# Where the C tiles stand in the second mixer's input projection

## The chip, the cores and the metric

The kernel runs on one core of a Trainium2 chip. One launch computes the whole step, and the metric is the device time of that launch in microseconds. Engines are named as in the profile: PE is TensorE's matrix multiply and PEld its weight load, DVE is VectorE, ACT is ScalarE, POOL is GpSimd and SP is the engine that issues most of the DMAs. In a profile row, "idle before <- X" says how long an engine stood still before the instruction, and who released it.

## What is computed

The reference is one inference step of a trunk with two layers: layer 0 mixes tokens with a long convolution (Hyena), layer 1 with a bidirectional Mamba-2 scan (SSD), and each is followed by an expert-choice mixture of experts. There are 128 context tokens and 1024 latent tokens, 9 tiles of 128 in all, with a model width of 1024. The change touches only the SSD mixer's input projection:

```python
proj = h @ in_w
z = proj[..., :SSD_D_INNER]
xbc = silu(_dwconv(proj[..., SSD_D_INNER:SSD_D_INNER + SSD_XBC], conv_w, conv_b))   # 5 taps along the tokens
dt_raw = proj[..., SSD_D_INNER + SSD_XBC:]
xh, bm, cm = split(xbc)            # 2048 columns of x, 4 groups x 128 of B, 4 groups x 128 of C
...
chunk_states = einsum('bcsgn,bcsgrp->bcgrpn', bm, xdt * decay_end[..., None])
s = s * dec[..., None, None] + st  # the recurrence over the chunks, forwards and backwards
y_off = einsum('bclgn,bcgrpn->bclgrp', cm, starts) * exp(a_cum)[..., None]
```

The states need B and x of a group, and not C. C and z are first used in the scan phase that comes afterwards.

## The kernel before

The program is a chain of phases with a barrier of all engines between them. `phase_ssd_in` is the projection. The output columns are cut into 40 tiles of 128 columns: 16 z tiles, 16 x tiles, 4 B tiles and 4 C tiles (`xbc_tile_of` numbers x as 0 to 15, B as 16 to 19, C as 20 to 23). They are worked through in the order q = 0 to 39. Three z tiles lead in. After them come four periods of nine tiles, one for each group g; `place(q)` gives the group and the position j in it. Position 0 is the group's B tile, positions 1 to 4 are its four x tiles, and what positions 5 to 8 hold is what the change is about. One tile is left over after the last period.

Work on a tile q, by engine:

- PE: 72 matmuls of 128x384 (`project`, recorded at L63, in the helper `product3`), in two halves with side work between (`middle(q)`) and behind (`end(q)`). Each product is made of three, from a leading and a trailing part of the weights and of h.
- A z tile: ACT evicts three banks with a SiLU in one instruction (`z_tile`, L3063), and POOL stores 576 KB to `z_dram` (L3337).
- An x, B or C tile: ACT evicts in three copies into a padded tile (L3072 to L3074) and computes the middle tap (L3079), DVE adds the other four taps one behind the other (`taps`, L3214), ACT takes the SiLU (L3087), and POOL stores 64 and 512 KB to `xbc_dram` (L3342, L3343). Of x and B tiles PE also makes transposes (`turn`, L2957), which ACT copies out (L3101, L3119).
- ACT and DVE split the weights of tile q+2 into their leading and trailing part (`lead`, L3058, and `rest`, L3205).

The states of a group run on the same engines as side work. At position 5, behind `taps(q)` and `rest(q+2)`, DVE decays the first state in both directions (`decay`, L3261) and weighs the x rows of the first chunk (`weigh`, L3248). In the middle of position 6 PE multiplies these with B (`contribute`, L2983); it waits there for `s_xw`, the semaphore that `weigh` raises. DVE then adds the product to the state (`add`, L3268), weighs the next chunk, and so on, two steps a tile: positions 6, 7 and 8 take steps 0 to 5, and position 0 of the next group takes step 6 and the context's own step (L2980, whose result ACT copies out at L3136 and SP stores in four DMAs at L2878).

The order on every engine is written out by hand: what an instruction waits for holds back all that is queued behind it on its engine. The phase ends when SP has seen all its stores land and POOL all of its own. Then the semaphores are cleared, all engines meet, and `phase_scan` begins with SP's first load (L3434).

Of the kernel before, what the change touches and what calls it, by code (L numbers as in the profile page):

```python
# [37 lines left out]
GROUPS = 4  # L38
XBC_TILES = 24
Z_TILES = 16  # L40
# [2632 lines left out]
LEAD_IN = 3  # L2673
# [5 lines left out]
def place(q):  # L2679

    return divmod(q - LEAD_IN, PERIOD)


def xbc_tile_of(q):

    if q < LEAD_IN:
        return None
    g, j = place(q)
    if g == GROUPS:
        return Z_TILES + 2 * GROUPS - 1  # L2690
    if j == 0:
        return Z_TILES + g
    if j <= 4:
        return 4 * g + j - 1
    if g == GROUPS - 1 and j >= 6:
        return Z_TILES + GROUPS + j - 6
    return None


def z_tile_of(q):  # L2700
    return q if q < LEAD_IN else LEAD_IN + 4 * place(q)[0] + place(q)[1] - 5


def tile_columns(q):
    x = xbc_tile_of(q)
    at = z_tile_of(q) * P if x is None else INNER + x * P
    return slice(at, at + P)


XBC_BEFORE = [sum(xbc_tile_of(p) is not None for p in range(q)) for q in range(TILES_IN + 1)]  # L2710

STORED_BEFORE = [sum(16 if xbc_tile_of(p) is None else 32 for p in range(q % 2, q, 2)) for q in range(TILES_IN + 2)]


# [36 lines left out]
def phase_ssd_in(nc, io, keep):  # L2751


    with ExitStack() as ctx:
# [91 lines left out]
        with nc.Block() as block:  # L2846
# [484 lines left out]
            @block.gpsimd  # L3331
            def _(pool):
                for q in range(TILES_IN):
                    x, s_done = xbc_tile_of(q), s_st[q % 2]
                    if x is None:
                        pool.wait_ge(s_ev, q + 1)
                        pool.dma_start(io["z_dram"][:, :, z_tile_of(q), :].rearrange("t p c -> p t c"),  # L3337
                                       out[:, q % 2, 0:TOK].rearrange("p (t c) -> p t c", c=P)).then_inc(s_done, 16)
                    else:
                        pool.wait_ge(s_si, XBC_BEFORE[q] + 1)  # L3340
                        group, at = (x // 4, x % 4) if x < Z_TILES else (x % 4, 4 + (x - Z_TILES) // 4)
                        pool.dma_start(io["xbc_dram"][0, :, group, at, :], out[:, q % 2, 0:P]).then_inc(s_done, 16)  # L3342
                        pool.dma_start(io["xbc_dram"][1:, :, group, at, :].rearrange("t p c -> p t c"),  # L3343
                                       out[:, q % 2, LAT_AT:].rearrange("p (t c) -> p t c", c=P)).then_inc(s_done, 16)
                    if q == LEAD_IN:
                        for n in range(3):
                            wait_taken(pool, U_ROWS + n)
                        pool.dma_start(io["row_dram"].rearrange("t r l -> r t l"),
                                       S(2).rearrange("p (t l) -> p t l", l=P)).then_inc(s_cr, 16)
                for b in range(2):  # L3350
                    pool.wait_ge(s_st[b], STORED_BEFORE[TILES_IN + b])
                pool.wait_ge(s_cr, 16)
# [507 lines left out]
```

## Time and profile before

| | us |
|---|---|
| median of 3 runs | 3690.69 (3690.11 to 3694.54) |
| the profiled execution's own time | 3688.76 |
| its span | 3687.0 |
| PE busy | 3384.2 (92%) |
| DVE busy | 1864.5 (51%) |
| ACT busy | 1278.0 (35%) |
| mean granted clock of TensorE | 0.951 of full speed |

The input projection lies between about 1790 and 2389 us of the span, the scan phase behind it. The granted clock is 1.00 where TensorE runs at 2.4 GHz and 0.50 at 1.2 GHz.

### The profile page before, as it was taken

The page shows a single profiled execution, that of the slowest core. Times are in us where ns is not written, and L with a number is a line of the kernel's source. Part 1 is how long each engine was busy: PE and PEld are TensorE (multiplying, and loading weights), DVE is VectorE, ACT ScalarE, POOL GpSimd, SP SyncE. Part 2 cuts the span into 40 slices and gives each one's busy share as a digit, 9 for nine tenths or more (in the row PEclk, how much of TensorE's full clock was granted, in tenths as well). Part 3 has the DMA queues.
Part 4 walks back from the last instruction along what each step waited for, and adds up shares of the span by engine and source line. Part 5 has one row for each costly group of instructions (what it writes and reads, how often), then busy time and mean ns, then how long its engine had stood idle before and what let it go on. Part 6 is the DMA issues. An engine that isn't in the chain of part 4 may idle for free. (4 is left out here: it accounts for less than half of the span.)

```text
span 3687.0 us, 58736 instructions
## 1 busy us (share of the span) xinstructions
PE 3384.2 (92%) x24055; PEld 2915.0 (79%) x24055; DVE 1864.5 (51%) x3039; ACT 1278.0 (35%) x2048; POOL 365.2 (10%) x356
## 2 busy tenths in 40 slices
PE   6999898977699999997899999789997499999998
PEld 5999674755599999996899999656664499999997
DVE  6333487765433333333455455599996533333334
ACT  4322323222133333333433233267664132232223
POOL 0000000000111111111010000000000011111111
PEclk8999898988799999998899999989998699999999
DMA  7666313254688888885143443497776488888887
GB/s 244 225 199 203 132 48 127 105 198 160 239 287 286 287 287 286 286 290 175 54 134 102 156 143 101 134 345 250 255 256 233 151 286 293 299 289 286 286 289 263
DMA packets 414015, 798.95 MB, mean 217 GB/s; under 512 B 21991, under 2 KB 108844, under 8 KB 412555
## 3 DMA queue, kind: packets, MB, share of 16 engines
q1 hardware_dynamic: 384940, 700.50, 54.1%
q0 software_dynamic: 28720, 96.31, 8.8%
q8 instruction: 102, 1.67, 0.2%
q14 instruction: 45, 0.37, 0.0%
q10 hardware_dynamic: 208, 0.10, 0.0%
HBM read 687.94 MB, written 108.90 MB: 216 GB/s over the span
## 5 line engine op out<-in xcount | busy, mean ns | idle before, releaser
L2438 PEld LDWEIGHTS moe_banks<-moe_xt,mix_ring 128*128 128x128 f32 x8192 | 1012.1, 191 | 5.7 <-issue 3.2
L2438 PE MATMUL moe_banks<-moe_xt,mix_ring 128*128 128x144 f32 x8192 | 1013.4, 287 | 3.1 <-ACT moe_xt L2482 3.1
L63 PE MATMUL ssd_banks<-h_leading,ssd_w_split 128*128 128x384 f32 x1920 | 417.3, 346 | 1.5 <-DVE ssd_w_split L3205 1.5
L2611 DVE TENSOR_TENSOR moe_hid<-moe_banks,moe_sg 128x128 f32<-128x128 f32 x256 | 74.6, 292 | 580.8 <-ACT moe_sg L2534 580.8
L2463 PE MATMUL moe_banks<-moe_down_parts,moe_hid_parts 128*128 128x512 f32 x1536 | 357.8, 392 | 0.0
L63 PEld LDWEIGHTS ssd_banks<-h_leading,ssd_w_split 128*128 128x128 f32 x1920 | 339.3, 189 | 16.1 <-issue 13.6
L2463 PEld LDWEIGHTS moe_banks<-moe_down_parts,moe_hid_parts 128*128 128x128 f32 x1536 | 285.9, 188 | 71.3 <-issue 13.2
L2554 DVE TENSOR_TENSOR moe_down_parts<-mix_ring,moe_down_parts 128x2048 fp32r<-128x2048 f32 x128 | 292.4, 2284 | 0.0
L3486 PE MATMUL scan_banks<-scan_w,scan_yc 128*128 128x512 f32 x576 | 255.0, 596 | 0.0
L2398 POOL DMA_INDIRECT x_dram<-moe_yc,mix_idx_quarter x128 | 166.3, 1299 | 830.7 <-DVE moe_yc L2622 801.5
L63 PE MATMUL hyin_early_banks<-h_leading,hyin_early_w_split 128*128 128x384 f32 x1152 | 245.0, 340 | 0.9 <-PEq L101 0.9
L2490 ACT ACTIVATE moe_down_parts<-mix_ring 128x2048 fp32r<-128x2048 f32 x128 | 242.9, 1897 | 0.0
L2534 ACT ACTIVATE moe_sg<-moe_banks 128x144 f32<-128x144 f32 x256 | 74.5, 291 | 427.2 <-PE moe_banks L2438 426.6
L63 PE MATMUL ssd_banks<-h_trailing,ssd_w_split 128*128 128x384 f32 x960 | 222.6, 338 | 0.0
L3214 DVE SCALAR_TENSOR_TENSOR ssdin_mid<-ssdin_pad,prm,ssdin_mid 128x1154 f32<-128x1154 f32 x96 | 136.4, 1421 | 156.5 <-ACT ssdin_mid L3079 154.0
L2534 ACT ACT_TABLE_LOAD x30 | 38.5, 1283 | 501.6 <-PE moe_banks L2438 501.6
L63 PEld LDWEIGHTS hyin_early_banks<-h_leading,hyin_early_w_split 128*128 128x128 f32 x1152 | 204.2, 189 | 2.8 <-issue 2.6
L3486 PEld LDWEIGHTS scan_banks<-scan_w,scan_yc 128*128 128x128 f32 x576 | 107.6, 192 | 122.3 <-issue 122.3
L2604 DVE SCALAR_TENSOR_TENSOR moe_yr<-moe_banks,mix_gate_lat,moe_g 128x512 f32<-128x512 f32 x64 | 48.0, 750 | 303.9 <-PE moe_banks L2463 298.8
L63 PEld LDWEIGHTS ssd_banks<-h_trailing,ssd_w_split 128*128 128x128 f32 x960 | 172.5, 189 | 0.0
L63 PE MATMUL hyin_early_banks<-h_trailing,hyin_early_w_split 128*128 128x384 f32 x576 | 137.3, 338 | 0.0
L1820 PE MATMUL hyout_banks<-hyout_w_parts,hyout_g_parts 128*128 128x512 f32 x432 | 104.4, 399 | 19.5 <-DVE hyout_g_parts L1856 19.5
(472 smaller groups left out, 4381.8 us busy)
## 6 DMA issues: line engine op xcount, KB each, us to landing
mix_ring<-in_moe_w_gate SPq DMA_DIRECT2D x64, 2048.0 KB, 8.0
mix_ring<-in_moe_w_up SPq DMA_DIRECT2D x64, 2048.0 KB, 12.9
mix_ring<-in_moe_w_down SPq DMA_DIRECT2D x64, 2048.0 KB, 8.7
early_ring<-in_ada_w SPq DMA_DIRECT2D x84, 512.0 KB, 6.6
scan_cum<-row_dram SPq DMA_DIRECT2D x36, 1024.0 KB, 6.6
ssd_w<-in_ssd_in_w SPq DMA_DIRECT2D x40, 512.0 KB, 4.2
s_dram<-ssdin_work SPq DMA_DIRECT2D x64, 256.0 KB, 3.6
scan_states<-s_dram SPq DMA_DIRECT2D x32, 512.0 KB, 7.9
```

What stands on the lines that cost most here:

```text
L63: ins = pe.matmul(out(piece), w_at(w[a], k), h_k(h[b], k, piece), start=(k == 0 and a == 0 and b == 0), stop=(k == KD - 1 and a == 1))
L1820: ins = pe.matmul(pb[:, 2 * (t % 2) + half, :], g_parts[:, t % 2, a, k, :], w_parts[:, b, k, half * HALF:(half + 1) * HALF], start=(k == 0 ...
L2398: pool.indirect_dma_start(io["x_dram"].rearrange("t (a c) -> (t a) c", a=4), bass.IndirectOffsetOnAxis(ap=keep["idx_quarter"][:, j, e:e + ...
L2438: ins = pe.matmul(pb[:, 2 * (f % 2) + j, 0:SLOTS], ring[:, 2 * half + j, k, col:col + P], xt[:, k, :], start=(k == 0), stop=(k == KD - 1))
L2463: ins = pe.matmul(pb[:, LAT_BANK[half], :], hid_parts[:, a, k, :], wd[:, half, b, k, :], start=(k == 0 and a + b == 0), stop=(k == KD - 1 ...
L2490: act.activation(wd[:, half, 0, ks, :], ring[:, 4 + half, ks, :], ACT.Copy).then_inc(s_wh, 1)
L2534: act.activation(sg[:, f % 2, :], pb[:, 2 * (f % 2), 0:SLOTS], ACT.Silu).then_inc(s_sg, 1)
L2554: dve.tensor_tensor(wd[:, half, 1, ks, :], ring[:, 4 + half, ks, :], wd[:, half, 0, ks, :].bitcast(F32), ALU.subtract).then_inc(s_wl, 1)
L2604: dve.scalar_tensor_tensor(yr[:, cols], pb[:, LAT_BANK[half], :], column("gate_lat", e), g2[:, cols], ALU.mult, ALU.mult).then_inc(s_yr, 1)
L2611: dve.tensor_tensor(hid[:, f % 2, :], up[:, 0:CAP_LAT], sg[:, f % 2, 0:CAP_LAT], ALU.mult).then_inc(s_hid, 1)
L3214: ins = dve.scalar_tensor_tensor(mid[:, b, :], pad[:, b, tap:tap + GAPPED], prm[:, 0, at:at + 1], mid[:, b, :], ALU.mult, ALU.add)
L3486: ins = pe.matmul(pb[:, out_bank(t) + half, :], yc[:, n % RING, j, :], w[:, k, half * HALF:(half + 1) * HALF], start=(k == 0), stop=(k == ...
```

## The change

Two functions are edited, `xbc_tile_of` and `z_tile_of`; all engines read the order of the tiles from them.

```diff
     g, j = place(q)
     if g == GROUPS:
-        return Z_TILES + 2 * GROUPS - 1
+        return None
     if j == 0:
         return Z_TILES + g
     if j <= 4:
         return 4 * g + j - 1
-    if g == GROUPS - 1 and j >= 6:
-        return Z_TILES + GROUPS + j - 6
+    if j == 5:
+        return Z_TILES + GROUPS + g
     return None
 
 
 def z_tile_of(q):
-    return q if q < LEAD_IN else LEAD_IN + 4 * place(q)[0] + place(q)[1] - 5
+    return sum(xbc_tile_of(p) is None for p in range(q))
```

Before, a period was B, x, x, x, x and four z tiles, except in the last group, where one z tile was followed by C, C, C and, as the left-over tile q = 39, the fourth C. Now each period is B, x, x, x, x, C and three z tiles, and q = 39 is a z tile. The counts are the same, 16 z tiles and 24 others, and so are all the instructions of PE, in number and kind.

On DVE, the end of the first group before (L3214 are the taps of a tile, L3205 the split of weights, L3261 and L3248 the first decay and the first weighing of the group's states, L3268 their first sum):

```order
L3214 SCALAR_TENSOR_TENSOR ssdin_mid<-ssdin_pad,prm,ssdin_mid 128x1154 x4
L3205 TENSOR_TENSOR ssd_w_split<-ssd_w,ssd_w_split 128x1024 x2
L3261 TENSOR_TENSOR ssdin_work<-ssdin_work,rates 128x512 x2
L3248 TENSOR_TENSOR ssdin_xw<-ssdin_work,rates 128x512 x2
L3268 TENSOR_TENSOR ssdin_work<-ssdin_work,ssd_banks 128x512 x2
```

and the same place after the change:

```order
L3214 SCALAR_TENSOR_TENSOR ssdin_mid<-ssdin_pad,prm,ssdin_mid 128x1154 x4
L3205 TENSOR_TENSOR ssd_w_split<-ssd_w,ssd_w_split 128x1024
L3214 SCALAR_TENSOR_TENSOR ssdin_mid<-ssdin_pad,prm,ssdin_mid 128x1154 x4
L3205 TENSOR_TENSOR ssd_w_split<-ssd_w,ssd_w_split 128x1024
L3261 TENSOR_TENSOR ssdin_work<-ssdin_work,rates 128x512 x2
L3248 TENSOR_TENSOR ssdin_xw<-ssdin_work,rates 128x512 x2
L3268 TENSOR_TENSOR ssdin_work<-ssdin_work,ssd_banks 128x512 x2
```

Four more taps stand ahead of the second weight split, and so ahead of the first decay and weighing. This holds in each of the four groups.

On ACT, the end of the phase before (L3072 to L3074 and L3079 evict a tile with taps, L3087 is its SiLU, L3136 the copy of the context's states):

```order
L3087 ACTIVATE ssdin_out<-ssdin_mid 128x1154
L3072 ACTIVATE ssdin_pad<-ssd_banks 128x128
L3073 ACTIVATE ssdin_pad<-ssd_banks 128x256
L3074 ACTIVATE ssdin_pad<-ssd_banks 128x768
L3079 ACTIVATE ssdin_mid<-ssdin_pad,prm 128x1154
L3136 ACTIVATE ssdin_ctx_state<-ssd_banks 128x512 x2
L3087 ACTIVATE ssdin_out<-ssdin_mid 128x1154
```

and after the change, where L3063 is the eviction of a z tile and L3058 ACT's part of a weight split:

```order
L3063 ACTIVATE ssdin_out<-ssd_banks 128x1152
L3058 ACTIVATE ssd_w_split<-ssd_w 128x1024
L3063 ACTIVATE ssdin_out<-ssd_banks 128x1152
L3058 ACTIVATE ssd_w_split<-ssd_w 128x1024
L3063 ACTIVATE ssdin_out<-ssd_banks 128x1152 x2
L3136 ACTIVATE ssdin_ctx_state<-ssd_banks 128x512 x2
```

The last tile's chain of eviction, taps and SiLU has become one eviction, and the copies of the context's states are the last thing that ACT does in the phase. POOL's last two stores to `xbc_dram` have become one to `z_dram`.

## Rows read from the trace of the kernel before

**Rows 1.** Windows (length; busy us PE, PEld, DVE, ACT, POOL; clock, DMA, GB/s)

```profile
2242.00:2312.00 70.00, 70.00 (x424) 69.69 (x423) 34.09 (x25) 31.04 (x47) 8.25 (x11) 1.00 0.31 96
2312.00:2344.00 32.00, 32.00 (x163) 28.13 (x162) 24.35 (x33) 8.61 (x13) 1.48 (x2) 1.00 0.50 176
```

**Rows 2.** Timeline of PE, last group (start us, duration us, engine, line, operation)

```profile
2316.01 1.88 PE L2983 MATMUL ssd_banks<-ssdin_xw,ssdin_brow 128*128 128x512 f32 x4
```

**Rows 3.** Timeline of DVE, positions 4 and 5 of the last group

```profile
2298.14 5.79 DVE L3214 SCALAR_TENSOR_TENSOR ssdin_mid<-ssdin_pad,prm,ssdin_mid 128x1154 f32<-128x1154 f32 x4 [7.02 <-ACT ssdin_mid L3079]
2303.84 1.22 DVE L3205 TENSOR_TENSOR ssd_w_split<-ssd_w,ssd_w_split 128x1024 fp32r<-128x1024 f32 x1
2312.06 1.23 DVE L3205 TENSOR_TENSOR ssd_w_split<-ssd_w,ssd_w_split 128x1024 fp32r<-128x1024 f32 x1 [7.00 <-ACT ssd_w_split L3058]
2313.20 1.29 DVE L3261 TENSOR_TENSOR ssdin_work<-ssdin_work,rates 128x512 f32<-128x512 f32 x2
2314.40 1.29 DVE L3248 TENSOR_TENSOR ssdin_xw<-ssdin_work,rates 128x512 f32<-128x512 f32 x2
```

**Rows 4.** Timeline of ACT, the same two positions

```profile
2295.46 0.28 ACT L3072 ACTIVATE ssdin_pad<-ssd_banks 128x128 f32<-128x128 f32 x1 [3.62 <-PE ssd_banks L63]
2308.97 1.14 ACT L3063 ACTIVATE ssdin_out<-ssd_banks 128x1152 f32<-128x1152 f32 x1 [3.67 <-PE ssd_banks L63]
```

**Rows 5.** Timeline of PE, start of the projection

```profile
1806.23 1.96 PE L2926 MATMUL ssd_banks<-tri,ssdin_work 64*128 64x64 f32 x16 [4.03 <-DVE ssdin_ones L3315]
...
1811.83 2.12 PE L63 MATMUL ssd_banks<-h_leading,ssd_w_split 128*128 128x384 f32 x6
1813.75 1.16 PE L63 MATMUL ssd_banks<-h_trailing,ssd_w_split 128*128 128x384 f32 x3
...
1816.73 1.20 PE L63 MATMUL ssd_banks<-h_leading,ssd_w_split 128*128 128x384 f32 x6
1817.77 0.68 PE L63 MATMUL ssd_banks<-h_trailing,ssd_w_split 128*128 128x384 f32 x3
```

**Rows 6.** Windows around three idle spells of PE

```profile
1802.20:1805.40 3.20, 0.00 (x0) 0.00 (x0) 3.10 (x4) 0.00 (x0) 0.00 (x0) 1.00 0.00 0
1805.40:1815.70 10.30, 7.92 (x35) 7.74 (x36) 4.29 (x12) 4.04 (x4) 2.18 (x2) 0.50 0.60 173
...
456.20:460.60 4.40, 0.03 (x1) 0.03 (x1) 4.33 (x5) 1.06 (x2) 0.00 (x0) 1.00 0.50 120
460.60:464.00 3.40, 3.40 (x8) 2.72 (x9) 3.40 (x4) 1.97 (x2) 0.00 (x0) 0.50 0.00 0
...
777.60:781.50 3.90, 3.90 (x9) 3.13 (x10) 3.90 (x4) 3.42 (x4) 0.00 (x0) 0.50 1.04 348
```

**Rows 7.** Timeline of ACT and POOL, end of the projection and one z tile

```profile
2372.07 0.28 ACT L3072 ACTIVATE ssdin_pad<-ssd_banks 128x128 f32<-128x128 f32 x1 [4.24 <-PE ssd_banks L63]
...
2374.61 1.06 ACT L3136 ACTIVATE ssdin_ctx_state<-ssd_banks 128x512 f32<-128x512 f32 x2
...
2310.39 0.99 POOL L3337 DMA_DIRECT2D z_dram<-ssdin_out  x1 [3.52 <-ACT ssdin_out L3063]
...
2382.57 0.90 POOL L3343 DMA_DIRECT2D xbc_dram<-ssdin_out  x1
```

**Rows 8.** Timeline of PE and SP, end of the projection

```profile
2371.87 1.95 PE L2980 MATMUL ssd_banks<-ssdin_brow,ssdin_xw 128*128 128x128 f32 x16
...
2375.21 2.90 SPq L2878 DMA_DIRECT2D out_new_state<-ssdin_ctx_state  x4
2389.64 0.38 SPq L3434 DMA_DIRECT2D scan_cum<-row_dram  x1
```

**Rows 9.** DMA issues, 2360 to 2389 us, then the whole run (last: us to landing)

```profile
xbc_dram<-ssdin_out POOLq DMA_DIRECT2D x2, 512.0 KB, 3.8
out_new_state<-ssdin_ctx_state SPq DMA_DIRECT2D x4, 128.0 KB, 2.4
...
z_dram<-ssdin_out POOLq DMA_DIRECT2D x16, 576.0 KB, 4.9
```

## The prediction

> **What bounds the kernel now.** I read the windows by stage first. In the last group, where the tiles still stand in their old order, PE is busy all the time at full clock: 70.00 of 70 us up to the first z tile's end, and 32.00 of 32 us where the C tiles begin [rows 1]. DVE has 24 of 32 us in the densest part and 34 of 70 in the other. So PE sets the time of the projection, its instructions aren't changed, and the only ways for this edit to move the time are to make PE stand still inside the phase, or to change what lies between PE's last matmul and the first load of the next phase. I therefore read two places in the timelines: the point at which PE first needs a group's weighed rows, and the end of the phase.
>
> At the first place PE comes to the contribution L2983 at 2316.01, with no idle time before it [rows 2]. DVE weighs both directions from 2314.40 for 1.29 us, so until 2315.69 [rows 3]. The slack is 0.3 us. At the second place PE is done at 2373.8 (2371.87 + 1.95), and SP's first load of the scan goes out at 2389.64 [rows 8]: 15.8 us in which PE has nothing.
>
> **Part 1: the C tile in position 5, four times.** The z tile there is evicted from 2308.97 [rows 4]. A tile with taps is evicted from the same point of its tile (position 4: 2295.46), and its taps begin on DVE at 2298.14, 2.68 us later [rows 3, 4]. So the C tile's taps begin at 2308.97 + 2.68 = 2311.65. From the taps' start to that of the weight split behind them is 5.70 us (2303.84 - 2298.14), from there to the decay 1.14 (2313.20 - 2312.06), from there to the weighing 1.20 (2314.40 - 2313.20), and the first of the two weighings takes half of 1.29, 0.65 [rows 3]. That ends at 2311.65 + 5.70 + 1.14 + 1.20 + 0.65 = 2320.3. PE wants it at 2316.0 and gets it 4.3 us later. The second weighing ends at 2321.0, when the first direction's two matmuls are just done, and adds nothing. ACT isn't late: its two copies of the last x tile come before its SiLU, and what it does behind that SiLU (the third copy, some 0.3 us) is over at about 2319, since the taps end at 2317.4.
>
> What is queued behind the waiting matmul on PE is the second half of position 6 and all that follows. PE has no slack in the phase to make it up in, since it is at 100% on both sides of the place; DVE, ACT and the weight loads move back with it. So 4.3 us a group are lost, four times: 17.2 us. Bounds: not under 3.7 (if the eviction or the copies in between go half a microsecond faster than in position 4), not over 5.0.
>
> **Part 2: the clock after such a wait.** The trace has a stall like this in the same phase: PE stood idle for 4.03 us before 1806.23 [rows 5], the clock was 1.00 up to 1805.4 and 0.50 until 1815.7, with 7.92 us of PE busy in it [rows 6]. Another, 4.4 us long, before 460.6: the clock then was 0.50 for 3.4 us of dense matmuls. At 777.6 dense matmuls began at the low clock and it took 3.9 us to rise [rows 6]. At the low clock six matmuls of 384 columns are 1.92 us apart (1813.75 - 1811.83), at the full one 1.04 (1817.77 - 1816.73) [rows 5], so a busy microsecond at the low clock loses 1 - 1.04/1.92 = 0.46 us. Bounds for each stall: nothing, if the clock holds; 7.92 x 0.46 = 3.6 us, as at 1806. There the first thing behind the idle time was 16 small transposes and a second wait of PE; here real matmuls follow without a hole, as at 460.6 and 777.6. I take 3.4 to 3.9 us, 1.6 us lost in each, 6.4 in all, and keep 0 and 14.4 as ends.
>
> The Trainium skill, page "TensorE: Matmul & The Clock Gate", section "Why this matters for your kernels", warns of gaps of more than about 3 us between bursts of matmuls, which speaks against this change; its section "What you observe" puts the return to full speed at about 4 us of sustained matmuls. By that rule each stall would lose 4 x 0.46 = 1.8 us and the sum below would be 0.8 us more; by the row at 1806, where it took 10.3 us, it would be 8 us more.
>
> **Part 3: the C tiles leave positions 6 to 8 of the last group.** DVE has 3 x 5.8 us less there. PE was at 100% with them [rows 1], so nothing is gained: DVE's busy time was beside PE's.
>
> **Part 4: the end of the phase.** Before, PE's last product went through ACT's eviction (from 2372.07), four taps on DVE and the SiLU, and POOL issued the last store at 2382.57 [rows 7]; with 3.8 us to landing [rows 9] it was there at 2386.4, and SP's first load followed at 2389.64, 3.2 us on. Now the last tile is evicted at 2372.07 in 1.13 us, and POOL issues its store 1.42 us after ACT's start (2310.39 - 2308.97) [rows 4, 7], at 2373.5. With the run's median of 4.9 us for such a store [rows 9] it lands at 2378.4. The other end is SP's: the context's states. They were copied from 2374.61 [rows 7] and stored by four DMAs from 2375.21, 0.73 us each, the last at 2377.4 [rows 8], landing 2.4 us later [rows 9]. ACT can now copy the first direction right behind the eviction, at about 2373.1 instead of 2374.61, and the second when PE's last matmul is done, 2373.9. That moves the last landing from 2379.8 to 2378.3. So both ends come out at 2378.4 where 2386.4 was before: 8.0 us gained. What is late next is these two together. Bounds: 6.0 (each is 2 us later, because the two stores and the last states share the DMA engines) and 9.0 (an undisturbed store lands after 3.8 us and the copies go earlier).
>
> **The sum.** 17.2 + 6.4 - 8.0 = +15.6 us. Against the profiled execution's 3688.8 us that gives 3704.4. The median of the runs is 1.9 us above the profiled one, so a median would be 3706.3; I say 3706. Everything outside this phase is unchanged.
>
> **Rivals.**
> 1. The clock stays low after each stall as long as at 1806. For it: that is the only stall of this size in this phase [rows 5, 6]. Against it: what PE did behind it. 17.2 + 14.4 - 8.0 = +23.6, so 3714.
> 2. The clock holds. For it: PE is fully busy up to the wait and after it. Against it: both idle spells of 4.0 and 4.4 us were followed by a low clock [rows 6]. 17.2 - 8.0 = +9.2, so 3700.
> 3. The other side, faster: the first weighing is in time, and only the shorter end remains. Its place is PE's wait before L2983, its price nothing, and it would give -8.0, 3683. It decides once the wait is under 2.0 us a group (8.0/4). For that the four taps would have to cost under 2.3 us of delay, with 0.3 of slack; they take 5.79 [rows 3] and stand ahead of the weighing on an engine that works in order. I see nothing that would carry them past it.
> 4. No measurable change: the wait is there but about half as long, because the eviction, taps and weighing overlap better than position 4 shows, and the clock holds: 4 x 2.5 - 8.0 = +2, 3693.
>
> **How the numbers follow.** The forecast has 0.64, rival 1 0.14, rival 2 0.11, rival 3 0.05 and rival 4 0.06. A measurement of this kernel can tell about 0.2%, 7.4 us, from no change. Slower than that are the forecast, rival 1 and most of rival 2: 0.87. Within it are rival 4 and a little of rival 2: 0.08. Faster: 0.05. The range takes in rivals 1 and 2 with the bounds of the end of the phase: low is 4 x 3.7 - 8.0 = +6.8, so 3697; high is 17.2 + 14.4 - 6.0 = +25.6, so 3716.
>
> **What would show it.** In the profile of the changed kernel, PE waits about 4.3 us for DVE's L3248 in front of L2983, four times, 17 us in all, and there is no such wait before. The first weighing of a group begins 5.3 us later against the end of position 5's matmuls than before. After each of the four waits the granted clock is 0.50 for 3 to 4 us of work. The last z store is issued 1.4 us after ACT's last eviction, and SP's first load of the scan comes about 8 us after PE's last matmul instead of 15.8. The forecast is wrong if PE isn't seen waiting at L2983, if the clock is low for much longer than 4 us, or if the barrier still comes some 15 us behind PE because another store is the last to land.

## The result and the profile after

The changed kernel takes 3712.69 us (median, 3711.16 to 3714.27), the one before 3691.35 us in the same measurement: a ratio of 1.0058, with a 95% interval of 1.0046 to 1.0069. It is 21 us slower. The forecast was 3706, the range 3697 to 3716. The profiled execution took 3712.92 us, 24.2 us more than the profiled one of before.

The waits of PE on the second mixer's projection, in total, have a new entry (engine, line, waited for; us in total, times, longest):

```profile
PE ssd_banks L2983 <- DVE ssdin_xw L3248: 17.8, 4, 4.5
```

Before there was no such entry. The PE timeline of the changed kernel shows the first of the four, in answer to [rows 2], and where the next contribution comes:

```profile
1921.28 0.27 PE L2957 MATMUL ssd_banks<-tri,ssdin_out 128*128 128x128 f32 x1
1926.01 3.75 PE L2983 MATMUL ssd_banks<-ssdin_xw,ssdin_brow 128*128 128x512 f32 x4 [4.46 <-DVE ssdin_xw L3248]
...
1936.18 1.88 PE L2983 MATMUL ssd_banks<-ssdin_xw,ssdin_brow 128*128 128x512 f32 x4
```

Here the reader is to see two losses. The idle time is 4.46 us. Then the half tile up to the next contribution takes 10.17 us (1936.18 - 1926.01), where the same stretch before took 7.98, as before's PE timeline shows:

```profile
1919.14 0.27 PE L2957 MATMUL ssd_banks<-tri,ssdin_out 128*128 128x128 f32 x1
1919.25 1.88 PE L2983 MATMUL ssd_banks<-ssdin_xw,ssdin_brow 128*128 128x512 f32 x4
...
1927.23 1.88 PE L2983 MATMUL ssd_banks<-ssdin_xw,ssdin_brow 128*128 128x512 f32 x4
```

The contribution started 0.11 us after the start of the transpose in front of it, while that was still running; now it starts 4.73 us after it. So the wait moves all that follows by 4.62 us, a little more than the idle time.

DVE at the same place, in answer to [rows 3]. The taps of the C tile now stand between the last x tile's and the first weighing, which begins at 1925.07:

```profile
1917.02 5.79 DVE L3214 SCALAR_TENSOR_TENSOR ssdin_mid<-ssdin_pad,prm,ssdin_mid 128x1154 f32<-128x1154 f32 x4 [6.58 <-ACT ssdin_mid L3079]
1922.73 1.22 DVE L3205 TENSOR_TENSOR ssd_w_split<-ssd_w,ssd_w_split 128x1024 fp32r<-128x1024 f32 x1
1923.87 1.28 DVE L3261 TENSOR_TENSOR ssdin_work<-ssdin_work,rates 128x512 f32<-128x512 f32 x2
1925.07 1.28 DVE L3248 TENSOR_TENSOR ssdin_xw<-ssdin_work,rates 128x512 f32<-128x512 f32 x2
```

The windows of the changed kernel show the clock (length; busy us of PE, PEld, DVE, ACT, POOL; granted clock, DMA share, GB/s). The first lies in the first half of the first wait; the second, fourth, fifth and sixth are the low spells of the four groups, and the third is all that lies between the first two of them:

```profile
1921.60:1923.50 1.90, 0.00 (x0) 0.00 (x0) 1.90 (x2) 0.65 (x1) 0.00 (x0) 1.00 0.00 0
1923.50:1930.30 6.80, 4.29 (x7) 2.25 (x8) 4.04 (x7) 0.68 (x2) 1.45 (x2) 0.50 0.75 247
1930.30:2063.40 133.10, 130.31 (x740) 123.94 (x738) 68.83 (x73) 42.27 (x61) 10.32 (x14) 1.00 0.37 121
2063.50:2070.20 6.70, 5.13 (x9) 3.10 (x10) 3.94 (x8) 0.00 (x0) 1.33 (x2) 0.50 0.87 305
2203.50:2210.20 6.70, 5.65 (x11) 3.61 (x12) 3.95 (x8) 0.00 (x0) 0.80 (x1) 0.50 0.95 338
2343.40:2350.10 6.70, 5.88 (x12) 3.84 (x13) 3.94 (x7) 0.00 (x0) 0.57 (x1) 0.50 1.02 352
```

The clock falls to 1.2 GHz while PE still stands: 2.5 us before PE goes on at the first wait (1923.50 and 1926.01), 0.8 us before at the last. It stays low for some 6.8 us each time, and so 4.29 to 5.88 us of PE's work fall into it, 20.95 in all. The end of the phase, in answer to [rows 7, 8], from the timelines of PE, ACT, POOL and SP:

```profile
2403.02 1.95 PE L2980 MATMUL ssd_banks<-ssdin_brow,ssdin_xw 128*128 128x128 f32 x16
...
2403.22 1.13 ACT L3063 ACTIVATE ssdin_out<-ssd_banks 128x1152 f32<-128x1152 f32 x1 [14.83 <-PE ssd_banks L63]
...
2404.65 1.00 POOL L3337 DMA_DIRECT2D z_dram<-ssdin_out  x1 [14.97 <-ACT ssdin_out L3063]
...
2404.86 3.76 SPq L2878 DMA_DIRECT2D out_new_state<-ssdin_ctx_state  x4
2413.07 0.38 SPq L3434 DMA_DIRECT2D scan_cum<-row_dram  x1
```

From PE's end (2404.97) to the first load of the scan it is now 8.1 us, where it was 15.8.

These account for the profiled difference. From L2926 near the start (1808.48 after, 1806.23 before) to L2980 at the end (2403.02 after, 2371.87 before) PE takes 594.5 us where it took 565.6: 28.9 us more. Of that 18.5 are the waits (4 x 4.62). The low clock can be read by itself, from the start of each delayed contribution to that of the next one: 10.17, 10.57, 10.78 and 10.92 us where 7.98 was before, 10.5 us more in all, or 0.50 us for each of the 20.95 busy us. The two make 29.0. The end gives 7.7 back. The remaining 3.0 us lie outside: 2.3 are there before L2926 is reached, in phases that are the same in both, and 0.7 behind the first load. The medians, 21.3 us apart, agree with 28.9 - 7.7 = 21.2.

### The profile page after: what moved, and what is told of

Its sections match the earlier page's. It is cut to its first block and busy times, and to the rows that moved or that the text cites. A ratio compares the mean times of both kernels' runs of the same rounds, so it can differ in the third digit from the quotient of the medians.

```text
span 3711.1 us, 58736 instructions
## 1 busy us (share of the span) xinstructions
PE 3390.5 (91%) x24055; PEld 2918.4 (79%) x24055; DVE 1865.5 (50%) x3039; ACT 1277.4 (34%) x2048; POOL 365.5 (10%) x356
## 5 line engine op out<-in xcount | busy, mean ns | idle before, releaser
L63 PEld LDWEIGHTS ssd_banks<-h_leading,ssd_w_split 128*128 128x128 f32 x1920 | 341.6, 190 | 18.3 <-issue 15.8
L3214 DVE SCALAR_TENSOR_TENSOR ssdin_mid<-ssdin_pad,prm,ssdin_mid 128x1154 f32<-128x1154 f32 x96 | 136.5, 1422 | 177.1 <-ACT ssdin_mid L3079 174.6
## 6 DMA issues: line engine op xcount, KB each, us to landing
mix_ring<-in_moe_w_up SPq DMA_DIRECT2D x64, 2048.0 KB, 12.8
```

The costliest lines, as they stand in the source:

```text
L63: ins = pe.matmul(out(piece), w_at(w[a], k), h_k(h[b], k, piece), start=(k == 0 and a == 0 and b == 0), stop=(k == KD - 1 and a == 1))
L3214: ins = dve.scalar_tensor_tensor(mid[:, b, :], pad[:, b, tap:tap + GAPPED], prm[:, 0, at:at + 1], mid[:, b, :], ALU.mult, ALU.add)
```

## The experiments

All kernels below were timed beside the kernel before. Its median was 3690.42 us beside the first four and 3692.21 us beside the last four. Times of different occasions are compared by their distances from it.

**C in the seventh place, a z tile last.**

```diff
-    if j == 5:
+    if j == 6:
         return Z_TILES + GROUPS + g
```

> Each group's C tile in the seventh place (position 6) instead of the sixth; a z tile is still last. My theory: the loss comes from the taps that stand ahead of a group's first weighing, so PE doesn't wait at L2983 at all, the clock doesn't fall inside the projection, and only the shorter end of the phase is left: 7 to 8 us faster than before, about 3684. Rival A, more taps beside the side work cost wherever they stand (DVE is the denser for it): PE waits in position 6 or 7 and the time stays above 3695. Rival B, the shorter end was worth nothing and the whole difference lies elsewhere: 3691, as before.

Measured: 3681.84 us, ratio 0.9978 (0.9969 to 0.9987). PE's waits have no entry for L2983, and the stretch that holds all four groups is at full clock, with PE busy all but 1.1 us of it (a wait of 1.15 us at 1851, which the kernel before has as well):

```profile
1820.00:2372.00 552.00, 550.86 (x3118) 521.17 (x3118) 288.51 (x311) 175.59 (x254) 48.64 (x62) 1.00 0.39 126
```

One place further on, the taps stand behind the weighings of the steps, as DVE's timeline shows. The first weighing (1918.68) is again in time, and 5.8 us of taps start at 1933.19, where DVE's next deadline is the weight split for a tile still to come:

```profile
1916.33 1.23 DVE L3205 TENSOR_TENSOR ssd_w_split<-ssd_w,ssd_w_split 128x1024 fp32r<-128x1024 f32 x1 [7.00 <-ACT ssd_w_split L3058]
1917.47 1.29 DVE L3261 TENSOR_TENSOR ssdin_work<-ssdin_work,rates 128x512 f32<-128x512 f32 x2
1918.68 1.29 DVE L3248 TENSOR_TENSOR ssdin_xw<-ssdin_work,rates 128x512 f32<-128x512 f32 x2
...
1933.19 5.79 DVE L3214 SCALAR_TENSOR_TENSOR ssdin_mid<-ssdin_pad,prm,ssdin_mid 128x1154 f32<-128x1154 f32 x4
```

So the sixth place is what costs, and rival A (taps beside side work cost anywhere) is out. With the waits gone, the shorter end shows as a gain of 8 us, and rival B is out too. This version beats both kernels.

**C in the sixth place, the weighing first.**

```diff
+                    if q >= LEAD_IN and place(q)[1] == 5:
+                        ... decay and weigh, both directions
                     if xbc_tile_of(q) is not None:
                         taps(q)
                     rest(q + 2)
-                    if q >= LEAD_IN and place(q)[1] == 5:
-                        ... decay and weigh, both directions
```

On ACT, `middle(q + 1)` goes ahead of `silu(q)` in the same position: with the old order the third copy of the last x tile would wait for the taps, and PE for that copy's bank.

> The changed order of tiles (C in the sixth place), but in position 5 DVE does a group's first decay and weighing ahead of the taps of the C tile, and ACT does the middle work of the next tile ahead of that tile's SiLU. My theory: the queue order on DVE alone makes PE wait, so the wait at L2983 is gone or under 0.5 us a group, and the time is 6 to 8 us under before, about 3684 to 3686. Rival A, it is the C tile's own work in that place that is too much for DVE or ACT: some of the wait comes back at L2983 or later, at the weight split, and the time is between 3693 and 3713.

Measured: 3682.34 us, ratio 0.9980 (0.9971 to 0.9989), and no wait at L2983. The tiles stand exactly as in the changed kernel; only DVE's and ACT's order within one position differs. DVE's timeline shows that the weighing now waits for ACT's copies of the x rows, and is done in time all the same:

```profile
1917.69 1.29 DVE L3252 TENSOR_TENSOR ssdin_xw<-ssdin_work,rates 128x512 f32<-128x512 f32 x2 [5.86 <-ACT ssdin_work L3119]
1918.91 5.78 DVE L3218 SCALAR_TENSOR_TENSOR ssdin_mid<-ssdin_pad,prm,ssdin_mid 128x1154 f32<-128x1154 f32 x4
```

So the cause is the order of the queues and not the amount of work. ACT's order was changed along with DVE's, but it isn't what made PE wait in the changed kernel: DVE's rows there run from the taps at 1917.02 to the weighing at 1925.07 without any idle time before an instruction.

**Three C tiles in the sixth place, the fourth last.**

```diff
     if g == GROUPS:
-        return None
+        return Z_TILES + 2 * GROUPS - 1
-    if j == 5:
+    if j == 5 and g < GROUPS - 1:
```

> C in the sixth place in groups 0 to 2 alone; the last group's C tile is the left-over tile q = 39, as before, so the long end of the phase is back. My theory: three waits of 4.5 us with 2 to 2.8 us of low clock each, 3 x 7.2 = +21, and an end of 15.8 us from PE's last matmul to the first load of the scan: about 3712, the same as the changed kernel, because one wait less and the lost end cancel. Rival, the end is worth nothing: 3 x 5.3 (a quarter each of the 21 us that were measured) = +16, about 3707.

Measured: 3711.11 us, ratio 1.0060 (1.0046 to 1.0073), with three waits of 4.5 us, 13.4 in all, and 15.4 us from PE's last matmul to the next load. The time is that of the theory (3712). The rival's 3707 lies at the edge of the interval, so the timing alone hardly excludes it; that the end is worth something is shown by the long end in this profile and by the seventh place with a C tile last, further down.

**The wait filled with work.** In the middle of position 6, 24 matmuls are added ahead of `contribute`; their results are overwritten unread.

```diff
+                    if j == 6:
+                        fill(q)
...
+                def fill(q):
+                    pe.wait_ge(s_ev, q)
+                    for n in range(24):
+                        pe.matmul(pb[:, bank(q + 1) + n % 3, 0:THIRD], split[:, q % 2, 0, n % 8, :],
+                                  third(keep["h_parts"][0], n % 8, n % 3), start=True, stop=True)
```

> The changed kernel with 24 more matmuls of 128x384 ahead of the first contribution of each group (96 in all), into banks whose results nobody reads, so that PE is busy for 24 x 0.173 = 4.2 us of the 4.5 it would wait. My theory: the wait itself can't be shorter, but the clock doesn't fall behind it; the 11 us that PE needs longer in the phase beside its waits are gone, and the time is about 3702. Rival, the low clock costs little and those 11 us are something else (contention, later waits): 3710 to 3713.

Measured: 3703.22 us, ratio 1.0033 (1.0021 to 1.0045), 13 us over its kernel before. It is 9.5 us under the changed kernel (3712.69), which was timed on another occasion; by the distances from the kernel before (12.8 and 21.3 us) it is 8.5. PE's timeline shows the added matmuls, the wait that is left (0.27 us) and the next tile at full speed:

```profile
1920.88 4.43 PE L3014 MATMUL ssd_banks<-h_leading,ssd_w_split 128*128 128x384 f32 x24
1925.58 1.96 PE L2983 MATMUL ssd_banks<-ssdin_xw,ssdin_brow 128*128 128x512 f32 x4 [0.27 <-DVE ssdin_xw L3256]
1926.97 1.09 PE L63 MATMUL ssd_banks<-h_leading,ssd_w_split 128*128 128x384 f32 x3
```

From 1820 to 2390 us the granted clock is 1.00. The contributions start as late as in the changed kernel (4.73 us after the transpose), and PE does 96 matmuls more, and yet the kernel is faster. From L2926 to L2980 PE takes 584.3 us, 10.2 less than in the changed kernel. That is the price of the low clock, and the rival (it costs little) is out. Contention with the DMAs, which are dense behind the wait in both kernels, is out as well: here the DMA engines are at least as busy as in the low spells above (a share of 1.03, against 0.75 to 1.02), and PE runs at full clock and without idle time:

```profile
1925.60:1932.00 6.40, 6.40 (x31) 5.44 (x32) 4.11 (x7) 0.00 (x0) 0.00 (x0) 1.00 1.03 378
```

**The wait half filled.** As above with `range(12)`.

> As the changed kernel with the filled wait, but only 12 added matmuls for each group, whose results nobody reads: PE is busy for 2.1 us of the 4.5 us, then idle for about 2.4 us. My theory, that the clock falls only behind a wait that is long enough, doesn't say where between 0.3 and 4.5 us that is. If the clock holds over 2.4 us: 3702, as with the full filling. If it falls each time as behind 4.5 us: about 3712. A value between would mean that it falls in some of the four.

Measured: 3705.11 us, ratio 1.0032 (1.0021 to 1.0044). Four waits of 2.4 us each are left, 9.5 in all. In the profiled execution the clock fell behind the first two and held over the other two. Windows of the two low spells, and of all that followed up to the end of the phase:

```profile
1923.60:1927.00 3.40, 3.08 (x5) 1.51 (x5) 1.36 (x3) 0.00 (x0) 0.08 (x1) 0.50 0.97 321
...
2063.50:2066.90 3.40, 3.40 (x9) 2.42 (x9) 2.52 (x5) 0.00 (x0) 0.00 (x0) 0.50 1.08 402
2066.90:2397.00 330.10, 324.15 (x1801) 303.49 (x1799) 169.13 (x193) 92.06 (x130) 27.47 (x34) 1.00 0.39 126
```

So a wait of 2.4 us is one that sometimes costs clock, and here the low spells were 3.4 us long, half of the changed kernel's. At the first the clock fell while PE stood, at the second 0.9 us after it had gone on at 2062.39. The time lies between the two that were expected, nearer to 3702; the timing alone doesn't tell it from the fully filled wait (both are 13 us over their kernel before).

**One C tile in the sixth place.** Groups 0 to 2 as before, the last group with C in positions 5 to 8, a z tile last.

```diff
-    if j == 5:
-        return Z_TILES + GROUPS + g
+    if g == GROUPS - 1 and j >= 5:
+        return Z_TILES + GROUPS + j - 5
```

> Groups 0 to 2 as before (four z tiles behind the x tiles), the last group with all four C tiles in positions 5 to 8, and a z tile last: one C tile in the sixth place instead of four. My theory: one wait of PE at L2983, 4.5 us, one fall of the clock worth 2.8 us on average, less the 7.8 us of the end: -0.5, so about 3690, no change that can be measured. Rival, the waits don't add up one by one (the later ones cost nothing, or the first costs it all): over 3695 or under 3685.

Measured: 3691.71 us, ratio 0.9998 (0.9989 to 1.0006). There is one wait of 4.5 us, and the end is short. With none (seventh place), one, and four waits the kernel is 8.6 us faster, level, and 21.3 us slower than the kernel before it was timed with: 8.1 us for the first wait, 7.3 for each of the next three. The interval of each of these times is about 3 us to either side, or more, so this only says that a single wait costs about as much as one of four; that it stood in the last group, with other C tiles behind it, made no difference that can be seen.

**C in the seventh place, but a C tile last.**

```diff
     if g == GROUPS:
-        return None
+        return Z_TILES + 2 * GROUPS - 1
-    if j == 6:
+    if j == 6 and g < GROUPS - 1:
```

> C in the seventh place in groups 0 to 2, and the last group's C tile as the left-over tile q = 39, as before. My theory: no wait of PE, no fall of the clock and the long end: 3690 to 3691, as before, 8 us over the version with a z tile last, so that the end alone is that version's gain. Rival, spreading the C tiles over the groups is itself worth something (DVE less dense in the last group): under 3687.

Measured: 3691.45 us, ratio 0.9996 (0.9988 to 1.0005), no wait, and 15.6 us between PE's end and the next load. Spreading the C tiles is worth nothing that can be measured by itself; the gain of 8 us is the last tile's.

**A quicker end, tried.** C in the seventh place, and for the last group the stores of one direction's context states issued by ACT (`store_ctx` holds the two DMAs that SP issued for a direction).

```diff
+                    if g == GROUPS - 1:
+                        wait_taken(act, step_unit(g, CTX_SLOT, 1))
+                        store_ctx(act, g, 1)
```

> C in the seventh place and, at the end of the phase, the stores of the second direction of the last group's context states issued by ACT right behind its copy instead of by SP behind two others. If SP's four stores, one behind the other, are what lands last in the shorter end: SP's part is done 1.9 us earlier and the first load of the scan comes 6.5 to 7.5 us behind PE's last matmul instead of 8.1, about 1 us less in all, 3681. If the z store lands last, or the DMA engines are the limit: no difference from the seventh place alone.

Measured: 3683.12 us, ratio 0.9974 (0.9963 to 0.9984), which can't be told from the seventh place alone (0.9969 to 0.9987). The issues of DMAs between 2370 and 2385 us show why (last column: us to landing):

```profile
out_new_state<-ssdin_ctx_state SPq DMA_DIRECT2D x2, 128.0 KB, 3.8
out_new_state<-ssdin_ctx_state ACTq DMA_DIRECT2D x2, 128.0 KB, 5.1
```

The four took 3.9 us in the seventh place alone. Issued about 1 us earlier, ACT's stores took longer, and the first load of the scan came at 2383.38, 8.0 us behind PE's end, where it was 8.1. So issuing them earlier brings nothing. Whether the z store that is in flight beside them holds them up, or the small stores themselves, wasn't separated; in the seventh-place kernel the DMA share is 0.91 in the 4 us from 2376 on.

## Why the prediction was right, and where its sizes were off

- **PE bounds the phase, without slack.** Right. It has no wait between 1852 and 2372 us in the kernel before, and what it lost in the four places it made up nowhere.
- **The wait.** Forecast 4.3 us, four times, 17.2; measured 4.62 and 18.5. The first weighing begins 5.3 us later against PE than before, as forecast. The missing 0.3 us is the time from the end of the first weighing (1925.07 + 0.64 = 1925.71) to PE's start at 1926.01, which I had left at nothing. The slack came out at 0.7 us (5.3 - 4.6) and not at the 0.3 that I named: I had counted that to the end of both weighings, and PE waits for the first alone: it starts before the second is done at 1926.35. The sum went by the first and isn't touched by it. That the queue order on DVE is the wait's cause was shown by the version with the weighing first; that ACT would not be late held in the changed kernel as it stands.
- **The clock.** The mechanism was right, and this is the term that was mis-sized: 1.6 us a wait, 6.4 in all, against 10.2 (by filling the waits) to 10.5 us (by the stretches behind the waits). Most of it is the length: I took the low spell as 3.4 to 3.9 us of work, from the two places where dense matmuls followed [rows 6], and it was 4.29 to 5.88 us of work here. The rest is the rate: a busy microsecond at the low clock lost 0.50 us, not 0.46, since the contributions at its start take 1.19 us each instead of 0.59, a larger ratio than that of the projection's matmuls. By the Trainium skill's page "TensorE: Matmul & The Clock Gate", section "What you observe", the return takes about 4 us of sustained matmuls. The windows above have 4.3 to 5.9 us, so for this kernel the page was nearer than my two rows, and still low. In the other versions the waits of 4.5 us were followed by 3.2 to 5.4 us of work at the low clock, and those of 2.4 us, where the clock fell, by 2.9 and 3.4. My upper end, 3.6 us lost a wait, was not reached.
- **The C tiles leaving positions 6 to 8 are worth nothing.** Right: shown by the seventh place with a C tile last, 3691.45 us.
- **The end.** Forecast 8.0 us, measured 7.7 in the profile, and 8 us by timing the seventh place with and without a z tile last (3681.84 and 3691.45, beside kernels before of 3690.42 and 3692.21). The way there was not as forecast, though: the context's stores took 4.0 us to land instead of 2.4 [rows 9], with the z store now in flight beside them, and SP needed 0.94 us to issue one instead of 0.73, as SP's row above (3.76 us for four) and the DMA issues of the changed kernel from 2403 to 2413 us show:

```profile
out_new_state<-ssdin_ctx_state SPq DMA_DIRECT2D x4, 128.0 KB, 4.0
```

  That is what I had given as the reason of my lower bound. By these numbers the last one lands at about 2411.7 (an estimate, 2404.86 + 3 x 0.94 + 4.0), 1.4 us ahead of the first load at 2413.07, where I had counted 3.2 us from the last landing to the load. Two errors of 1.5 to 2 us cancelled, so that this term came out so well is in part luck.
- **The sum.** +15.6 against +21.3. Of the 5.7 us that are missing the clock accounts for 4.1 (10.5 - 6.4), the waits for 1.3 and the end for 0.3. The time lies inside the range because the range allowed for a low spell like the one at 1806.
- **The rivals.** The clock held in none of the four; the first weighing was not in time; the waits were not half as long. Rival 1 (as long a low spell as at 1806, 3714) came nearer to the measured time than the forecast did, but not for its reason: the low spell was 6.8 us, not 10.3.

## What to carry to other kernels

When work is moved to another place of an order written by hand, look on each engine at what it is now queued ahead of, and at that instruction's slack, before adding up busy times: DVE was half idle here, and 5.8 us of taps still cost PE 4.5 us, since they were put ahead of the one instruction with 0.7 us of slack. One place further on they cost nothing. A wait of TensorE can cost more than itself: here a wait of 4.5 us cost about 7 us (4.6 by itself and 2.6 by the low clock behind it). At the end of a phase, order the tiles so that the one with the shortest chain behind TensorE comes last.

## What the runs showed of the hardware

- The granted clock fell at each of eight waits of 4.5 us inside dense work (four, three and one in the three kernels that have them), at two of four of 2.4 us, and at none of four of 0.3 us. It mostly fell while PE still stood, in the changed kernel 0.8 to 2.5 us before PE went on.
- Work that nobody reads made the kernel faster: 96 more matmuls in the place of idle time took 8.5 to 9.5 us off, because PE went on at 2.4 GHz.
- The low spell was 6.8 us long at six of the eight waits of 4.5 us, and 3.4 at the other two (one of three with the fourth C tile last, and the kernel with a single wait) and at both waits of 2.4 us. What it costs goes by how much of it PE works through: 2.9 to 5.9 us here, at about half a microsecond lost for each. What sets its length was not found out.
